# A residual kept with tokens on partitions, and output and down projections that stream 512 weight columns

## What is computed

```python
def reference(x, ...):
    for i in range(DEPTH):
        h = rms_norm(x, norm_mix[i])
        if i % N_MIXERS == 0:   # silu(layer_norm(dwconv31(glu(h @ w_in + b_in)))) @ w_out + b_out
            mix = conformer_conv(h, ...)
        else:                   # (softmax(q1 k1) - lam softmax(q2 k2)) v, rms_norm by head, @ w_o
            mix = diff_attention(h, positions, ...)
        x = x + mix
        h = rms_norm(x, norm_ffn[i])
        x = x + conv_ffn(h, ...)  # (silu(dwconv3(h @ w_gate)) * (h @ w_up)) @ w_down
    return rms_norm(x, norm_final)
```

## Time and profile before

| what | us |
| --- | --- |
| runs | 2238.19, 2249.48, 2249.57 |
| median | 2249.48 |
| the profiled execution, its own time | 2238.06 |
| its span | 2236.2 |
| TensorE busy in it | 2188.6 (98%) |
| VectorE busy | 1604.8 (72%) |
| ScalarE busy | 991.7 (44%) |
| HBM traffic | 393.6 MB, 176 GB/s on average |

### The profile page before, as it was taken

How to read it: one execution, slowest core, us unless ns; L and a number is a source line. 1 busy time by engine, 2 the same in 40 slices (tenths; PEclk the granted TensorE clock), 3 DMA queues, 4 the chain that set the end, 5 groups by cost and what they waited for, 6 DMA issues and landing times.

```text
span 2236.2 us, 36151 instructions
## 1 busy us (share of the span) xinstructions
PE 2188.6 (98%) x12078; PEld 1904.0 (85%) x12078; DVE 1604.8 (72%) x2695; ACT 991.7 (44%) x1450; POOL 32.9 (1%) x50
## 2 busy tenths in 40 slices
PE   8999799999999999999999998999999999999998
PEld 6888688888888888888888877888888888888887
DVE  7999977777777775555688866777777777764543
ACT  3000455444444444444444444554444444444443
POOL 5000000000000000000000000000000000000000
PEclk9999999999999999999999999999999999999999
DMA  7545466766666666676666555566666666666663
GB/s 199 153 136 147 113 169 178 197 190 188 188 188 188 189 188 182 185 188 182 189 181 169 174 170 163 146 183 182 186 187 188 188 185 184 182 180 186 183 176 114
DMA packets 742333, 393.60 MB, mean 176 GB/s; under 512 B 6471, under 2 KB 732529, under 8 KB 742257
## 3 DMA queue, kind: packets, MB, share of 16 engines
q1 hardware_dynamic: 742016, 392.92, 64.0%
q10 hardware_dynamic: 272, 0.09, 0.0%
HBM read 390.89 MB, written 2.10 MB: 176 GB/s over the span
## 4 chain that ended last, share of the span: by engine, by line
PE 96%; DVE 1%; SPq 1%; DMA 1%; ACT 1%; issue 1%; ACTq 0%; DVEq 0%
PE acc L1259 53%; PE acc L1261 27%; PE acc L1295 9%; PE acc L1477 1%; PE acc L1479 1%; PE acc L1478 1%; DMA sb_stage<-in_conv_w_in 1%; PE aux L1488 0%; SPq L297 0%; PE aux L1435 0%; PE aux L1347 0%; DVE sb_heads_op L744 0%; PE aux L1306 0%; PE aux L1303 0%; DVE sb_v_tok L1157 0%
## 5 line engine op out<-in xcount | busy, mean ns | idle before, releaser
L1259 PE MATMUL acc<-sb_normed,sb_w_hi 128*128 128x512 f32 x3264 | 1145.8, 396 | 0.0
L730 DVE TENSOR_TENSOR sb_w_lo<-sb_stage,sb_w_hi 128x1024 fp32r<-128x1024 f32 (+2 forms) x696 | 830.4, 1193 | 415.4 <-ACT sb_w_hi L446 404.7
L446 ACT ACTIVATE sb_w_hi<-sb_stage 128x1024 fp32r<-128x1024 f32 (+2 forms) x696 | 718.3, 1033 | 587.3 <-PE acc L1261 535.5
L1261 PE MATMUL acc<-sb_normed,sb_w_lo 128*128 128x256 f32 x3264 | 914.7, 280 | 0.0
L1259 PEld LDWEIGHTS acc<-sb_normed,sb_w_hi 128*128 128x128 f32 x3264 | 612.0, 188 | 143.6
L1261 PEld LDWEIGHTS acc<-sb_normed,sb_w_lo 128*128 128x128 f32 x3264 | 616.5, 189 | 0.3
L1259 PE MATMUL acc<-sb_hidden,sb_w_hi 128*128 128x512 f32 x1376 | 488.1, 398 | 0.0
L1261 PE MATMUL acc<-sb_hidden,sb_w_lo 128*128 128x256 f32 x1376 | 387.3, 281 | 0.0
L1259 PEld LDWEIGHTS acc<-sb_hidden,sb_w_hi 128*128 128x128 f32 x1376 | 258.3, 188 | 63.2
L1261 PEld LDWEIGHTS acc<-sb_hidden,sb_w_lo 128*128 128x128 f32 x1376 | 259.4, 189 | 0.0
L1295 PE MATMUL acc<-sb_x_op,sb_stage 128*128 128x256 f32 x1024 | 225.6, 381 | 1.3 <-DMA sb_stage<-in_conv_w_in 1.3
(11 more groups left out here) (170 smaller groups left out, 1339.1 us busy)
## 6 DMA issues: line engine op xcount, KB each, us to landing
sb_stage<-in_ffn_w_gate SPq DMA_DIRECT2D x86, 1024.0 KB, 5.7
...
```

The costliest lines, as they stand in the source:

```text
L446: nc.scalar.activation(w_hi[:, (2 * first + h) % PIECES, 0:size], stage[:, first % STAGES, off:off + size], ACT.Copy).then_inc(hi_ready, 1)
L730: nc.vector.tensor_tensor(w_lo[:, slot, 0:size], stage[:, first % STAGES, off:off + size], w_hi[:, slot, 0:size].bitcast(F32), ALU.subtrac ...
L1259: nc.tensor.matmul(acc[:, bank, :], w_hi[:, slot, q * P:(q + 1) * P], operand[:, k, :], start=begin, stop=end, skip_group_check=True)
L1261: return nc.tensor.matmul(acc[:, bank, T:2 * T], w_lo[:, slot, q * P:(q + 1) * P], operand[:, k, 0:T], start=False, stop=end, skip_group_c ...
```

## The change

The residual now has tokens on partitions: `resid` is [128, 2, 2048]. conv_out, down0, wo and down1 take the wide form of the value projection: a chunk is 512 outputs and two banks, a block is four k-tiles of 512 columns, and a down projection has 11 blocks a chunk (the last with three k-tiles). The interleaved start is gone. The weights are read from memory as 4 x 512 columns a partition.

VectorE takes a chunk out of PSUM with two additions of 512 columns (`evict`). TensorE then turns it by 8 transposes (`turn_resid`), which stand in the middle of the first block of the next chunk, or of the next stage; ScalarE and VectorE read the turned tiles in PSUM to make `normed`. ScalarE squares `resid` with a sum along the row (`squares`), and the sum of squares is one number a token: VectorE adds the parts (`row_squares`), ScalarE takes the root of 2 numbers a partition, VectorE inverts it and scales two identity matrices (`row_scales`, `diag_row`), which TensorE multiplies by ones (`stat`) to spread them over the partitions; VectorE copies the result out of PSUM (`rms`). In down1 nothing is turned: the gain of the final norm is multiplied in along the row (`regain`), and the stores read `resid`. The bias of conv_out and the final gain come as rows that are broadcast to 128 partitions, 1 MB each. The input lands in `resid` directly; ScalarE and VectorE share the scaling of its turned tiles.

```diff
-        resid = sb("resid", [P, KD, T])
...
+        resid = sb("resid", [P, TB, D])
...
+                sp.dma_start(gain_rows[:, :], norm_final.rearrange("(b d) -> b d", b=1).to_broadcast([P, D])
+                             ).then_inc(gain_loaded, 16)
...
+            def squares(n, c, unit0):
...
+                for b in range(TB):
+                    act.wait_ge(evacuated, BANKS + unit0 + TB * c + b + 1)
...
+                    nc.scalar.activation(square[:, :], resid[:, b, WIDE * c:WIDE * (c + 1)], ACT.Square,
+                                         accum_out=sq_parts[:, n, b, c:c + 1]).then_inc(squared, 1)
             def rms_root(n):
-                act.wait_ge(stat_ready, n + 1)
-                nc.scalar.activation(rms_t[:, :], aux[:, 3, T:2 * T], ACT.Sqrt, bias=const[:, 0:1],
+                act.wait_ge(sq_ready, n + 1)
+                nc.scalar.activation(row_scale[:, n, :], sq_sum[:, n, :], ACT.Sqrt, bias=const[:, 0:1],
                                      scale=1.0 / D).then_inc(root_ready, 1)
...
+            def norm_hi(n, c, gain):
+                for f in range(4):
+                    k = 4 * c + f
+                    act.wait_ge(resid_turned, 4 * CH * (n - 1) + k + 1)
+                    operand(0, normed[:, k, 0:T], aux[:, f, 0:T], par_d[:, gain * KD + k:gain * KD + k + 1], 0)
...
+                        if j == 0 and c > 0:
+                            squares(n, c - 1, C[name])
+                        if m + 2 < BLOCKS:
+                            hi(0, (0, m + 2), 0)
+                        if j == 0 and c > 0 and gain is not None:
+                            norm_hi(n, c - 1, gain)
+                        if m + 2 < BLOCKS:
+                            hi(0, (0, m + 2), 1)
+                        if c == CH - 1 and j == 0:
+                            warm_up(ACT.Sqrt)
+                squares(n, CH - 1, C[name])
+                if gain is not None:
+                    norm_hi(n, CH - 1, gain)
+                rms_root(n)
...
+            def row_squares(n):
+                dve.wait_ge(squared, TB * CH * (n + 1))
+                nc.vector.tensor_reduce(sq_sum[:, n, :], sq_parts[:, n, :, :], AX.X, ALU.add).then_inc(sq_ready, 1)
+            def row_scales(n, last=False):
+                dve.wait_ge(root_ready, n + 1)
+                nc.vector.reciprocal(row_scale[:, n, :], row_scale[:, n, :]).then_inc(rms_ready, 1)
+                dve.wait_ge(rms_ready, n + 1)
+                if not last:
+                    for b in range(TB):
+                        nc.vector.tensor_scalar(diag_row[:, b, :], ident[:, :], row_scale[:, n, b:b + 1], None,
+                                                ALU.mult).then_inc(diag_row_ready, 1)
...
             def rms(n):
-                dve.wait_ge(root_ready, n + 1)
-                nc.vector.reciprocal(rms_t[:, :], rms_t[:, :]).then_inc(rms_ready, 1)
-                nc.vector.memset(sq_sum[:, :], 0.0).then_inc(sq_added, 1)
-                dve.wait_ge(rms_ready, n + 1)
+                dve.wait_ge(stat_ready, n + 1)
+                own.mark(nc.vector.tensor_copy(rms_t[:, :], aux[:, 3, T:2 * T]))
+                own.wait()
...
-            def residual_chunk(i, blocks_per_turn, block_n, chunk_n, m, bias):
-                bank = chunk_n % BANKS
-                dve.wait_ge(pieces_done, 2 * blocks_per_turn * i + 2 * block_n + 2)
-                own.mark(nc.vector.scalar_tensor_tensor(out=summed[:, 0, :], in0=acc[:, bank, T:2 * T], scalar=bias,
-                                                        in1=resid[:, m, :], op0=ALU.add, op1=ALU.add))
-                own.wait()
-                nc.vector.tensor_tensor(resid[:, m, :], acc[:, bank, 0:T], summed[:, 0, :],
-                                        ALU.add).then_inc(evacuated, 1)
-                dve.wait_ge(evacuated, 4 * i + chunk_n + 1 + BANKS)
...
-                if not last:
-                    low_part(normed[:, m, :], resid[:, m, :], par_d[:, bass.ds(gain * KD + m, 1)],
-                             OPER[name] + 4 * i + j + 1)
...
+            def add_bias(c):
...
+                    ins = nc.vector.tensor_tensor(resid[:, b, WIDE * c:WIDE * (c + 1)],
+                                                  resid[:, b, WIDE * c:WIDE * (c + 1)],
+                                                  bias_rows[:, WIDE * c:WIDE * (c + 1)], ALU.add)
...
+            def evict(name, c):
+                n = STAT[name]
+                dve.wait_ge(pieces_done, 2 * (B[name] + NB[name] * (c + 1)))
+                for b in range(TB):
+                    cols = resid[:, b, WIDE * c:WIDE * (c + 1)]
+                    unit = C[name] + TB * c + b
+                    nc.vector.tensor_tensor(cols, acc[:, unit % BANKS, :], cols, ALU.add).then_inc(evacuated, 1)
...
+                for c in range(CH):
+                    for j in range(NB[name]):
+                        m = B[name] + NB[name] * c + j
+                        if j == 0 and c > 0:
+                            evict(name, c - 1)
+                        if m + 2 < BLOCKS:
+                            lo(0, (0, m + 2), 0)
+                        if j == 0 and c > 0 and gain is not None:
+                            norm_low(name, c - 1, gain)
+                        if m + 2 < BLOCKS:
+                            lo(0, (0, m + 2), 1)
+                        if j == 1 and c > 0 and gain is None:
+                            regain(c - 1)
+                        if c == 0 and bias:
+                            add_bias(j)
...
+                evict(name, CH - 1)
+                row_squares(STAT[name])
+                if gain is not None:
+                    norm_low(name, CH - 1, gain)
...
+                    if first is not None and e == 0:
+                        row_scales(STAT[first])
...
+                        row_scales(STAT["down0"])
                         rms(STAT["down0"])
-                        nc.vector.reciprocal(v_rms[:, :], v_rms[:, :]).then_inc(v_rms_ready, 1)
...
+            row_scales(STAT["down1"], True)
+            for b in range(TB):
+                cols = resid[:, b, D - WIDE:D]
+                nc.vector.scalar_tensor_tensor(out=cols, in0=cols, scalar=row_scale[:, STAT["down1"], b:b + 1],
+                                               in1=gain_rows[:, D - WIDE:D], op0=ALU.mult,
+                                               op1=ALU.mult).then_inc(tail_scaled[b], 1)
...
+                            wide = slice(WIDE * q, WIDE * (q + 1))
+                            for b in range(TB):
+                                bank = (first + b) % BANKS
+                                high, low = operand[:, k, b * P:(b + 1) * P], operand[:, k, T + b * P:T + (b + 1) * P]
+                                nc.tensor.matmul(acc[:, bank, :], high, w_hi[:, slot, wide], start=k == 0, stop=False)
+                                nc.tensor.matmul(acc[:, bank, :], high, w_lo[:, slot, wide], start=False, stop=False)
+                                ins = nc.tensor.matmul(acc[:, bank, :], low, w_hi[:, slot, wide], start=False,
+                                                       stop=k == tiles - 1)
+                        ins.then_inc(pieces_done, 1)
...
+            def turn_resid(name, c):
+                n = STAT[name]
+                pe.wait_ge(evacuated, BANKS + C[name] + TB * (c + 1))
+                if c > 0:
...
+                for f in range(4):
+                    k = 4 * c + f
+                    for b in range(TB):
+                        ins = nc.tensor.transpose(aux[:, f, b * P:(b + 1) * P], resid[:, b, k * P:(k + 1) * P],
+                                                  ident[:, :])
+                    ins.then_inc(resid_turned, 1)
...
-            def stat(n, sq):
-                pe.wait_ge(sq_added, sq)
-                nc.tensor.matmul(aux[:, 3, T:2 * T], ones[:, :], sq_sum[:, :], start=True,
-                                 stop=True).then_inc(stat_ready, 1)
+            def stat(n):
+                pe.wait_ge(diag_row_ready, TB * (n + 1))
+                for b in range(TB):
+                    ins = nc.tensor.matmul(aux[:, 3, T + b * P:T + (b + 1) * P], ones[:, :], diag_row[:, b, :],
+                                           start=True, stop=True)
+                ins.then_inc(stat_ready, 1)
...
+                arrivals = [(0, OPER[name] - 4)] + [(KD - 4 + f, OPER[name] - 3 + f) for f in range(4)]
+                block_mm(0, 4, B[name], C[name], normed, arrivals, lambda: turn_resid(before, CH - 1))
+                stat(STAT[before])
...
             def last_heads(k):
-                if k == 3:
+                if k == 2:
                     outputs(last, 0)
+                    outputs(last, 1)
+                elif k == 4:
+                    o_stats(last, 0)
                 elif k == 5:
-                    o_stats(last, 0)
-                elif k == 6:
-                    outputs(last, 1)
-                elif k == 9:
                     o_stats(last, 1)
```

539 lines of the change are left out of this document (222 added, 317 removed).

## The result

The changed kernel took 2277.79 us (median of 4 executions, 2269.19 to 2278.15) against 2249.53 before: 1.0134 times as long by the comparison of all the runs, with an interval of 1.0097 to 1.017 (the two medians alone give 1.0126). The forecast was 2260.2, "just inside what counts as no change"; the range went to 2280. So the range held the time, but only by 2 us; the forecast itself was 17.6 us too low, and the kernel is slower by 1.3%, clear of the noise, where the forecast called it unchanged within 0.5%.

A forecast was written before the change was run, and what follows sets the result against it. TensorE, busy 98% of the span and 96% of the chain, was taken as the bound. Terms summing to +10.7 on the profiled 2238.06 us gave 2248.8; an 11.4 us offset to the median made 2260.2, range 2236 to 2280.

The forecast's parts named there:

- rate of the wide form: Four projections: 0.3398 us of wide matmuls replace each 0.3533 us pair, over 1888 pairs: -25.6 us.
- 12 turns: Transposing finished chunks: 2.05 us each, including a 1.1 us wait for VectorE's evictions: +24.6 us.
- start of conv_out: Dropping the interleaved start saves 4.3 us, but block 2's low part comes late, +1.8: together -2.5 us.
- statistic product, up0 and up1: First block of both up stages: TensorE waits 2.3 us each for the diagonals: +4.6 us.
- statistic product, query stage: Query projection's first block: 3.9 us wait for the diagonals, then 1.5 us at halved clock: +5.4 us.
- wo: Start of wo: waits of 2.3 for the second sum and 2.4 for block 2, less savings: +2.9 us.
- start of the kernel: The input's diagonal stands behind the lambda work, so block 2 starts later: +2.4 us, between 0 and 4.
- lower clock: Of four new waits of 2.3 to 2.4 us, two lower TensorE's clock at 1.5 us each: +3.0 us.
- Rival 3: No gain in rate: the 0.2265 us belongs to one stretch, 0.235 stays, the 25.6 are gone: 2286 us; chance 0.13.
- rival 4: The broadcast loads run on one DMA engine, 40 us per 1 MB: +60, 2320 us; chance 0.04.
- Rivals 1: Waits hidden: evictions and diagonals are ready when TensorE asks, no clock lost: -21.7, so 2228 us; chance 0.13.
- rival 2: More waits: low clock follows each of the four waits and some of the 12 turns: 2262 to 2270; chance 0.28.

The follow-up runs named there:

- e4: e1 with the turns moved to the start of the second block of the next chunk, except each stage's last chunk: 2235.67 us, 0.9953 times before.
- e12: e8 with ScalarE and VectorE work at the start of wo reordered, and VectorE's evictions put ahead of the last low part: 2209.56 us, 0.9837 times before.
- e5: The changed kernel with 96 unused bytes ahead of conv_op, heads_op and hidden, putting them at 128 modulo 256: 2249.17 us.
- e1: The changed kernel with 32 unused bytes ahead of conv_op, heads_op and hidden, putting them at 64 modulo 256: 2256.69 us, 1.0027 times before.
- e3: The changed kernel with 32 unused bytes ahead of normed, putting normed at 160 and the other operand tiles at 64 modulo 256: 2246.17 us.
- e7: e4 with normed at 160, the other operand tiles at 128 modulo 256, and roots, reciprocals and diagonals made earlier: 2221.02 us, 0.9902 times before.
- e11: The changed kernel with 64 unused bytes ahead of conv_op, heads_op and hidden, putting them at 96 modulo 256: 2268.79 and 2277.35 us.
- e2: The kernel before with 32 unused bytes, moving hidden from 96 to 128 modulo 256, with conv_op and heads_op: 2232.2 us, 0.9914 times before.
- e6: The kernel before with normed, conv_op, heads_op and hidden all at 160 modulo 256: 2218.03 us, 0.9892 times before.
- e10: The kernel before with 96 unused bytes ahead of normed, putting normed at 224 and the other operand tiles at 192 modulo 256: 2240.65 us.
- e8: e7 with the input's root, reciprocal and diagonals ahead of the lambda work at the start of the kernel: 2218.95 us.

## Why the prediction was right or wrong

Its terms against what the two traces show (us). Rate, turns, waits and clock are read from rows; the other terms are what is left of the difference of their stage:

| term | forecast | measured |
| --- | --- | --- |
| rate of the wide form | -25.6 | -6.2 |
| 12 turns | +24.6 | +24.6 |
| turning of the result gone | -3.6 | -3.1 |
| start of conv_out | -2.5 | -2.8 |
| statistic product, up0 and up1 | +4.6 | +3.6 |
| statistic product, query stage | +5.4 | +5.0 |
| wo | +2.9 | +2.9 |
| start of the kernel | +2.4 | +5.7 |
| lower clock | +3.0 | +1.7 |
| end | -0.5 | -0.3 |
| sum | +10.7 | +31.1 |
| pair rate of up0 (not in the forecast) | 0 | +9.1 |

The spans differ by 39.9; 31.1 and 9.1 make 40.2. The offset of 11.4 between the profiled execution and the median, which the forecast added without knowing what it was, is for its larger part these 9.1: up0 of the profiled execution was fast, and by the steps of 9 the median execution has both up stages slow. Of the 17.6 us that the forecast was too low, the sum makes 20.4, 19.4 of them by the rate alone; the offset, 11.4 where 9.1 came, gives 2.3 back.

- **The rate is the step that failed.** "The new form ... 1.5 x 0.2265 = 0.3398 us": 0.2333 was measured, 0.3500 for the same work, 1888 x 0.0033 = 6.2 us. The value projection's matmul was read as what a wide matmul costs; it was what one costs whose stationary tile lies at 128 modulo 256. Rival 3 said that the rate might belong to the one stretch that shows it, with a chance of 0.13; its 0.235 came near for a reason that it did not name. The rule of the Trainium skill that stood there, "TensorE: Matmul & The Clock Gate", section "Back-to-back issue gap" (2.5 ns above the columns, which the section gives as the gap of an isolated matmul), would have given 2.4 us and fits none of the rates here, which lie 13 to 21 ns above the columns. There was a sign in the traces of before: pairs took 0.3533 on hidden and 0.3467 on normed, with the same code, and 0.3533 again in up1. I took the first as the price of a pair and did not ask why the other was less. At each form's best rate the wide form gains 1888 x 0.0067 = 12.6 us, half of what was forecast.
- **The turns** waited as was said, but that the term agrees to the tenth is luck. 62.13 us between two turns less 258 x 0.2333 leaves 1.93 (0.9 wait, 1.03 work) for the 2.05 forecast, 23.2 for twelve; 1.4 more came from the first turn, which waited 2.23, for a reason that the prediction had put at nothing. "The bias additions ... lie behind this on VectorE, with more than 3 us of slack, and cost nothing": the last two of them stood directly ahead of the first evictions.

```profile
310.01 1.29 DVE L949 TENSOR_TENSOR sb_resid<-sb_resid,sb_bias_rows 128x512 f32<-128x512 f32 x2
311.34 1.29 DVE L961 TENSOR_TENSOR sb_resid<-acc,sb_resid 128x512 f32<-128x512 f32 x2
...
312.77 1.94 PE L1294 MATMUL aux<-sb_ident,sb_resid 128*128 128x128 f32 x8 [2.23 <-DVE sb_resid L961]
```

  They took 1.3 us, and this wait is 1.4 longer than the others; no run moved them alone, so the rows are all that speaks for it. The clock at 0.50 behind it (1.7 us, below) came with it in this execution. The order that made the other waits (split at T+0.2, low part, evictions, TensorE on at T+3.9, with T at 933.89) stands in the rows of the turn of down0; e4 and e12 show that they go when the order does. The order of e12 was missing in the prediction.
- **First block after a projection.** The waits were 1.49, 1.48 and 3.34 for 2.3, 2.3 and 3.9: ScalarE took less time over the operand tiles. ScalarE's next split of weights, which VectorE's low part and then the reciprocal waited for, had ended at T+7.3 in up0 and not at T+8.0. The clock was at 0.50 for 3.2 us behind the one of 3.34, as said, and at 1.00 behind those of 1.5, 2.06 and 2.09. The stretch behind the longest:

```profile
1131.90:1135.10 3.20, 3.20 (x12) 2.72 (x11) 2.70 (x9) 0.00 (x0) 0.00 (x0) 0.50 1.00 285
```

  In e5 the same wait of 3.34 left it at 1.00:

```profile
1110.70:1113.90 3.20, 3.20 (x20) 2.85 (x21) 2.36 (x8) 0.00 (x0) 0.00 (x0) 1.00 0.80 233
```

- **wo** waited 2.06 for the second sum and 2.09 for block 2, for 2.3 and 2.4. Its +7.9 is 5.8 of turns, -0.85 of rate and the 2.9.
- **The start** was mis-sized, and outside its bounds of 0 to 4. TensorE waited 6.1 us for the diagonal, as the mechanism said, but then ran at half the clock for ten microseconds and not for three. The same stretch after:

```profile
32.70:42.80 10.10, 9.17 (x35) 7.62 (x36) 7.78 (x18) 1.84 (x3) 9.08 (x13) 0.50 0.27 66
```

and before:

```profile
32.70:42.80 10.10, 10.10 (x40) 8.58 (x40) 9.87 (x19) 1.92 (x3) 9.08 (x13) 0.83 0.24 67
```

  "The clock was low there before too" counted a change in how long as none. The prediction's own times (block 2 at 35 to 36 for 32.50) also gave 2.5 to 3.5 and not 2.4. The 5.7 is that of one pair of executions: with the same start, the changed kernel and e1, e3, e4, e5, e7 and e11 reach conv_out at 280.2 to 282.0, and the kernel before, e2, e6 and e10 at 275.7 to 277.3.
- **The lower clock.** Of the four waits that were counted, none of those between 1.48 and 2.09 lowered it; one turn did, the first of conv_out with 2.23. Two at 1.5 were forecast, one at 1.7 came. Which waits lower the clock is not the kernel's alone: behind the wait before the second sum of wo, 2.06 to 2.09 us in eight traces, the clock was at 1.00 in four (the changed kernel, e4, e8, e11) and at 0.50 in four (e1, e3, e5, e7). That the term came within 1.3 us is luck. The stretch in e1:

```profile
1437.50:1440.70 3.20, 3.20 (x9) 2.44 (x9) 2.51 (x3) 0.59 (x3) 0.00 (x0) 0.50 0.00 0
```

- **The end and the two broadcasts** were as said. The loads of 1 MB landed 7.8 and 6.7 us after their issue, and not the 40 of rival 4.
- **The rivals.** Rivals 1 and 4 did not happen, and of rival 2 only one turn at the lower clock did. The mechanisms of the likeliest case did, but without most of its gain, and the range held the time, by 2 us, because it took in half of rival 3. That is luck more than foresight: the rate lost three quarters of its gain, 19.4 us, and the bound stood 19.8 above the forecast.
